# Where the modulation vectors of a conditioned decoder trunk are summed: two units moved behind a norm's sum of squares

## The reference, cut to what matters

```
c_act = silu(c)                                  # one vector of 1024
mod = c_act @ w_mod[l] + b_mod[l]                # 6 x 1024: sh1, sc1, gt1, sh2, sc2, gt2
h  = rmsnorm(x, norm1_g) * (1 + sc1) + sh1
z  = h @ w_in;  ... three token mixers ...
x  = x + gt1 * (merged @ w_out)
h2 = rmsnorm(x, norm2_g) * (1 + sc2) + sh2
x  = x + gt2 * (gelu(conv(h2 @ w_up)_gate) * conv(h2 @ w_up)_val) @ w_down
```

## Time and profile before

| | |
|---|---|
| median of three runs | 1196.32 us |
| the profiled execution's own time | 1199.33 us |
| its span, first to last instruction | 1197.5 us |
| PE busy | 1151.9 us, 96% |
| DVE busy | 842.9 us, 70% |
| ACT busy | 567.7 us, 47% |
| mean granted clock of TensorE | 0.978 of full speed |

### The profile page before, as it was taken

One profiled execution on the slowest core, in us unless ns is written; L12 is line 12 of the kernel. 1 busy time (PEld: TensorE's weight loads), 2 busy tenths in 40 slices (PEclk: granted clock), 3 DMA queues, 4 the chain that ended last, 5 costly groups with the idle time before them and its releaser, 6 DMA issues.

```text
span 1197.5 us, 24198 instructions
## 1 busy us (share of the span) xinstructions
PE 1151.9 (96%) x10160; PEld 1043.8 (87%) x10160; DVE 842.9 (70%) x1246; ACT 567.7 (47%) x867; POOL 60.2 (5%) x104
## 2 busy tenths in 40 slices
PE   6999999999999999999999899999999999999997
PEld 6889888888788999999988698778887889999996
DVE  5468988477475788885535679876765767888763
ACT  2236547622264666652331274575124556666532
POOL 0000010003000000001000000000030000000000
PEclk9799999999999999998999899999999999999999
DMA  9956454234135466667725435441521545445650
GB/s 378 297 204 217 176 177 189 94 142 143 72 141 212 156 242 218 227 226 278 281 85 186 173 142 189 156 183 72 199 86 71 189 190 184 175 178 187 225 184 36
DMA packets 40951, 214.34 MB, mean 179 GB/s; under 512 B 7680, under 2 KB 8064, under 8 KB 21536
## 3 DMA queue, kind: packets, MB, share of 16 engines
q1 hardware_dynamic: 29344, 171.13, 39.0%
q0 software_dynamic: 11520, 41.95, 10.0%
HBM read 212.01 MB, written 1.05 MB: 178 GB/s over the span
## 4 chain that ended last, share of the span: by engine, by line
PE 83%; DVE 11%; issue 3%; DMA 3%; ACT 1%; SPq 0%; DVEq 0%; ACTq 0%
PE ps L1587 13%; PE ps L1589 13%; PE ps L1588 13%; PE ps L1600 8%; PE ps L1762 6%; PE ps L1760 6%; PE ps L1766 6%; PE ps L1864 4%; DVE RLO L1091 2%; DMA mring<-wmod_dram 2%; PE ps L1558 2%; PE ps L1565 2%; DVE macc L987 2%; PE ps L1549 1%; PE ps L2040 1%
## 5 line engine op out<-in xcount | busy, mean ns | idle before, releaser
L845 ACT ACTIVATE WH<-ring 128x1024 fp32r<-128x1024 f32 x144 | 151.6, 1058 | 185.7 <-PE ps L1589 170.0
L1459 DVE TENSOR_TENSOR WLO<-ring,WH 128x1024 fp32r<-128x1024 f32 x144 | 175.1, 1223 | 91.2 <-ACT WH L845 91.2
L1587 PE MATMUL ps<-HH,WH 128*128 128x256 f32 x736 | 208.3, 283 | 0.0
L1588 PE MATMUL ps<-HL,WH 128*128 128x256 f32 x736 | 208.3, 283 | 0.0
L1589 PE MATMUL ps<-HH,WLO 128*128 128x256 f32 x736 | 208.3, 283 | 0.0
L1587 PEld LDWEIGHTS ps<-HH,WH 128*128 128x128 f32 x736 | 141.3, 192 | 0.0
L1588 PEld LDWEIGHTS ps<-HL,WH 128*128 128x128 f32 x736 | 141.3, 192 | 0.0
L1589 PEld LDWEIGHTS ps<-HH,WLO 128*128 128x128 f32 x736 | 141.3, 192 | 0.0
L1587 PE MATMUL ps<-GH,WH 128*128 128x256 f32 x384 | 110.6, 288 | 0.0
L1588 PE MATMUL ps<-GL,WH 128*128 128x256 f32 x384 | 109.4, 285 | 0.0
L1589 PE MATMUL ps<-GH,WLO 128*128 128x256 f32 x384 | 109.4, 285 | 0.0
(11 more groups left out here) (383 smaller groups left out, 2494.5 us busy)
## 6 DMA issues: line engine op xcount, KB each, us to landing
ring<-wmain_dram SPq DMA_DIRECT2D x150, 1024.0 KB, 4.8
mring<-wmod_dram POOLq DMA_DIRECT2D x80, 512.0 KB, 5.0
G<-wmod_dram SPq DMA_DIRECT2D x3, 1024.0 KB, 7.8
R<-wmod_dram SPq DMA_DIRECT2D x3, 1024.0 KB, 15.6
TK<-wmod_dram SPq DMA_DIRECT2D x2, 1024.0 KB, 20.7
X<-x_t_dram SPq DMA_DIRECT2D x1, 1024.0 KB, 9.8
SW<-small_dram SPq DMA_DIRECT2D x2, 512.0 KB, 12.6
y_dram<-H SPq DMA_DIRECT2D x4, 256.0 KB, 2.2
```

The source lines that it names most:

```text
L845: A(WH[:, n % 2, part], ring[:, b, part], ACT.Copy).then_inc(hi_ready, 1)
L1459: V.tensor_tensor(WLO[:, n % 2, part], ring[:, b, part], WH[:, n % 2, part].bitcast(F32), ALU.subtract).then_inc(lo_ready, 1)
L1587: MM(out, w_high[:, at], high, start=start, stop=False, skip_group_check=True)
L1588: MM(out, w_high[:, at], low, start=False, stop=False, skip_group_check=True)
```

## The change

Units 3 and 4 change places in the order of units (and 9 and 10): scale 2 comes ahead of shift 2. `mod_row` and `mod_part` map a unit to its rows in the array of weights and biases; the number, the size and the order of the loads stay the same. The scale is then summed where the shift was, and the shift (units 4 and 10) is summed after `out(3, 0, KT)`, where `keep_clock(7, ...)` stood; four of its seven matmuls stay behind it. Unit 7 is no longer summed in the down-projection but after its end, again with four of the seven matmuls behind it. On DVE, `mod_vector(6 * l + 4)` moves from between `gated(4)` and `out_low(0)` to between the residuals and the norm; `mod_vector(7)` moves from ahead of the last four residuals of layer 0 to just ahead of the first norm of layer 1. The second half of the transposes now waits for one unit fewer.

```
+def mod_part(u):
+    return (0, 1, 2, 4, 3, 5)[u % 6]
+
+def mod_row(n):
+    return 48 * (n // 48) + 8 * mod_part(n // 8) + n % 8
...
-DN_SUMS = [{0: 5, 3: 6, 10: 7}, {8: 11}]
+DN_SUMS = [{0: 5, 3: 6}, {8: 11}]
... POOL
-                    pool.dma_start(mring[:, n % 2, :], wmod[n]).then_inc(s_m[n % 2], 16)
+                    pool.dma_start(mring[:, n % 2, :], wmod[mod_row(n)]).then_inc(s_m[n % 2], 16)
... ACT
-                shifts(2 * l + 1, 3 if l == 0 else 9)
+                shifts(2 * l + 1, 4 if l == 0 else 10)
... DVE
-                V.tensor_tensor(mod[:, u, :], ps[:, 6 if u == 1 else 7, 0:8], col(lay, "bmod", 8 * (u % 6), 8), ALU.add).then_inc(mod_ready, 1)
+                V.tensor_tensor(mod[:, u, :], ps[:, 6 if u == 1 else 7, 0:8], col(lay, "bmod", 8 * mod_part(u), 8), ALU.add).then_inc(mod_ready, 1)
...
                     norm_gain(col(l, "n1g", 0, 8), 0)
+                if l:
+                    mod_vector(7)
                 norm(2 * l, Acol)
...
                 gated(4)
-                mod_vector(6 * l + 4)
                 out_low(0)
...
-                norm_gain(col(l, "n2g", 0, 8), 4 if l == 0 else 10)
+                norm_gain(col(l, "n2g", 0, 8), 3 if l == 0 else 9)
                 for j in range(4):
                     if j >= 2:
                         low(0, j - 2)
                     residual(PAIRS * l + OU + j, j, sm[:, FH:FH + 8])
+                mod_vector(6 * l + 4)
                 norm(2 * l + 1, Acol)
-                u = 3 if l == 0 else 9
+                u = 4 if l == 0 else 10
... PE
                 pe.wait_ge(gn_rt, 2 * (l + 1))
-                mod_sum(6 * l + 4)
...
                     if half:
-                        pe.wait_ge(mod_ready, 6 * l + 5)
+                        pe.wait_ge(mod_ready, 6 * l + 4)
...
                 out(3, 0, KT)
-                keep_clock(7, 6, C[:, 0:S])
+                mod_sum(6 * l + 4)
+                keep_clock(4, 6, C[:, 0:S])
...
                 if l == 0:
-                    keep_clock(7, 6, C[:, 0:S])
+                    mod_sum(7)
+                    keep_clock(4, 6, C[:, 0:S])
```

## The result

The changed kernel takes 1184.74 us (median of four runs, 1182.28 to 1186.16); the kernel before, on the same chip, takes 1196.96 us (four runs, 1192.1 to 1201.09). The ratio is 0.9897, with an interval of 0.9855 to 0.994. The profiled execution's own time is 1185.98 us with a span of 1184.2 and a mean granted clock of 0.985 (before: 1199.33, 1197.5 and 0.978).

What follows compares the result with a forecast made beforehand. PE, busy for 96% of the span, was taken to bound the kernel. 3.2 (units 4 and 10) + 4.7 (unit 7) - 1.8 (clock falls in gaps) = 6.1 us less, from 1196.32 to 1190.2; range 1186.0 to 1195.5.

Steps and rivals of the forecast that it cites:

- the own places: Places the change itself touches: the merge in both layers, the end of layer 0, three norm gaps; forecast 6.1 us less.
- The first rival: In the three norm gaps the clock holds, so they are free: 7.9 us less, 1188.4 us; chance 0.22.
- Units 4 and 10: At the merge of each layer, removing the unit's 1.70 us sum from PE saves 1.6 us, 3.2 together.
- The margin at the transposes: After the merge, DVE's second pair of sums ends 0.19 us before the transposes' new start; 0.1 taken off for weight loading.
- Unit 7: End of layer 0: the last pair starts at 597.00 instead of 601.69, saving 4.7 us; 3.0 if the clock doesn't fall.
- The new wait of DVE: In the norm gaps, DVE's unit instruction ends before ACT's root releases the norm, with 0.46 us to spare.
- The clock of the gaps: In two of the three norm gaps the clock falls, at a mean price of 0.88 us: 1.8 us back.
- The start value: Whole kernel: the saving is taken from 1196.32, the median of the runs shown, 3.0 below the profiled execution, giving 1190.2.

Runs made afterwards that it cites:

- experiment 4: Kernel before with only DVE's instruction for unit 7 moved to ahead of the next norm, PE's sum left in the down-projection: 1192.8 us, ratio 0.9991.
- experiment 7: Changed kernel with the four fillers of each gap ahead of the unit's sum instead of behind it: 1191.25 us, ratio 0.9983.
- experiment 5: Changed kernel with no filler matmuls in the three gaps: 1186.93 us, ratio 0.9948.
- experiment 6: Changed kernel with seven instead of four filler matmuls behind the unit in each gap: 1187.62 us, ratio 0.9951.
- experiment 10: Changed kernel with unit 6 summed after down-projection pair 5 instead of pair 3, run twice: 1184.39 and 1183.35 us, ratios 0.99 and 0.9904.
- experiment 9: Both kernels profiled again, no edit: kernel before 1193.23, 1199.04 and 1189.35 us; changed kernel 1184.53, 1180.02 and 1183.65 us.

## Why the prediction was wrong, point by point

**All runs together.** The changed kernel has a mean of 1184.3 +-0.7 (40 runs, 1176.2 to 1194.2), the kernel before 1193.9 +-0.4 (113 runs, 1185.7 to 1205.5). The change is worth 9.6 +-0.8 us. The forecast time was 5.5 us too high, and this splits into four: 2.4 because it started from 1196.32, a median of three runs, where the mean is 1193.9; 2.0 because the own places give 8.1 (8.3, less 0.15 for falls of the clock in the gaps) and not 6.1; 1.5 +-0.8 that the runs show beyond the own places; less 0.4, as the changed kernel's first four runs lie that much above its mean.

The first rival, which had the clock right, gave 1188.4, so it too is 3.7 us too high.

**Units 4 and 10, right.** Forecast 1.6 each, measured 1.74 to 1.78 in five profiles. The margin at the transposes went as read, and it costs nothing to speak of, so the 0.1 taken off for it was not lost.

**Unit 7, right.** Forecast 4.7 with 3.0 as the other bound; measured 4.72 in all five profiles against the first one of before, 4.54 to 4.77 against the other three. That the ones matmuls ran at half clock was no accident of one execution: the low clock stands at this place in all four profiles of the kernel before (from 598.3, 592.5, 597.8 and 590.5 us). The split is shown by experiment 4.

**The new wait of DVE, right.** 0.46 us of cover, forecast and measured; experiment 7 shows the price without it, 1.18.

**The clock of the gaps: the step that failed.** It was "I take a fall in two gaps of three, at the mean price of the three: 1.8 us back". The price was near: forecast 0.5, 1.65 and 0.5 for the three gaps, measured 0.24, 1.69 and 0.29 in experiment 5. The frequency was wrong: 2 falls in 15 gaps, 0.4 us each, so 0.15 us for an execution where the sum has 1.8. I had set the one stretch of 20.8 to 24.9, where the clock fell behind 16 one-column instructions, against three gaps that had never been run this way, and gave a single row the weight of a rate. Nor was that stretch quite like the gaps: PE's timeline of the kernel before has more one-column instructions just ahead of its first fillers and behind its last ones, which the gaps don't have:

```profile
19.76 1.14 PE L1549 MATMUL ps<-sm,R 128*128 128x1 f32 x9
...
24.37 0.79 PE L1549 MATMUL ps<-sm,R 128*128 128x1 f32 x6
```

The row wasn't misleading in kind: with no fillers, with fourteen, or with the fillers first, the clock fell in 3, 2 and 2 of three gaps, one profile each. The rule of the Trainium skill, "TensorE: Matmul & The Clock Gate", section "HAM oscillation", to avoid the longer idle gaps of TensorE, would have given the first rival, which is what the changed kernel did in 13 of 15 gaps; but it isn't borne out as a rule here, since fill without idle time (experiment 6: PE busy from 597.92 to the product) lost the clock as well. Why eight fillers held it in 13 of 15 gaps in one kernel, and in 3 of 6 in experiment 10's, is open.

**The start value and the range: too narrow by their own data.** The larger single part of the miss, 2.4 us, is the step "the difference carries over, so I forecast 1190.2": it rests on 1196.32 as the kernel's usual time, and 113 runs show 1193.9. It took 2 us for the error of a median, from three runs that lay 5.5 apart. Executions of this kernel lie up to 20 us apart, and the median of a few moves with them. Within one kernel time follows the mean granted clock, 10 to 13.5 us for each 0.01. On lines fitted for each chip, at a clock of 0.985 the two kernels run at 1190.4 to 1190.9 and 1183.3 to 1184.0, some 7 us apart. I read that as the change's own work without its part in the clock, but no run shows it apart.

**What stays open.** Of the 1.5 us beyond the own places, experiment 9 shows where it would be. The stretch near 670 us is worth 1.7 and parts the two kernels in all nine profiles; the prediction had no term for it, and why the change brings it about isn't shown. The start, where 17 against 6.8 us is worth about 5 us, differs by the execution. At a standard error of 0.8 the 1.5 may also be chance.

## What to carry to other kernels

Put a small reduction where PE idles anyway, if its reader waits there for something that comes later still: the timeline shows both releases, and their distance (here 0.46 us) is the cover. An instruction that holds a queue costs more than its own length: 1.7 us of PE's sum cost 4.7, since DVE's residuals stood behind it. Where the clock of TensorE falls in some executions only, take its frequency from several profiles and the starting time from many runs, and make the range as wide as they lie apart.

## What the runs showed of the hardware beside this

- A float32 sum over partitions of a 128 x 8 result, 16 one-column instructions, takes 1.70 us between dense products at full clock, 0.106 each, where a filler of 256 columns takes 0.216: a 256th of the columns, half of the time.
- The start of one and the same kernel has a stretch at half clock of 6.8, 17.1 or 20.5 us, by the execution. In the Trainium skill, "TensorE: Matmul & The Clock Gate", section "What's actually happening", the count of slow matmuls at a kernel's start varies between runs of the same kernel and is worth less than 1% of a typical one. The stretch here isn't the first work of the kernel, as the granted clock was 1.00 for 13.6 us ahead of it in the changed kernel. In size it agrees: 20.5 us at half clock cost at most 10.3 us of 1191.4, 0.86%. It is no small thing all the same: the change is worth 0.8%.
- A stretch at half clock can stand at the same code in every profile of one kernel and in none of a near relative: 16 matmuls of 256 columns near 670 us take 5.33 us in four profiles of four before, 3.64 in five of five after the change, though the change doesn't touch them.
